# Output stage on grid columns, with the second Fourier step tile by tile

## The reference

```python
q, k, v, gA, bB, cB, hB, gB, uC, gC, qD, kD, vD, gD, aF, aB = split(hN @ w_in)
yA = attention(q, k, v) * silu(gA)           # 8 x 16 window of the grid, and 512 cached keys
yB = bB * conv3(cB * hB) * silu(gB)          # along the tokens, rows of the grid one after the other
yC = real(fft2(uC over tokens, over 64 channels)) * silu(gC)
yD = rms_norm(scan_forward + scan_backward) * silu(gD)
y  = x + gate * (concat(yA, yB, yC, yD) @ w_out)
```

## Time and profile before

| | us |
|---|---|
| median of 3 runs | 2692.43 (2691.7 to 2694.59) |
| the profiled execution | 2692.42 |
| its span, first to last instruction | 2690.7 |
| TensorE busy in it | 2508.2 (93%) |
| DVE, ACT, POOL busy | 1258.3, 990.2, 747.9 |
| DMA traffic | 395.37 MB, mean 147 GB/s |

### The profile page before, as it was taken

One profiled execution on the slowest core, in us unless ns is written; L12 is line 12 of the kernel. 1 busy time (PEld: TensorE's weight loads), 2 busy tenths in 40 slices (PEclk: granted clock), 3 DMA queues, 4 the chain that ended last, 5 costly groups with the idle time before them and its releaser, 6 DMA issues. The chain is left out here.

```text
span 2690.7 us, 53206 instructions
## 1 busy us (share of the span) xinstructions
PE 2508.2 (93%) x18956; PEld 2033.1 (76%) x18956; DVE 1258.3 (47%) x2620; ACT 990.2 (37%) x2031; POOL 747.9 (28%) x1147
## 2 busy tenths in 40 slices
PE   3899999999999969999999996989899985999999
PEld 1788888888888748888888885777777763888887
DVE  2544344344344343232323224667676753665654
ACT  1544544544444432222222213556565642111110
POOL 2233333333333210000000003433233332444442
PEclk8999999999999979999999998999999997999999
DMA  7533433433433362222222218887677768666563
GB/s 294 162 106 123 129 107 121 124 110 124 120 116 116 93 237 95 84 95 82 96 82 96 89 54 164 173 180 166 156 167 166 192 172 312 217 209 208 200 214 129
DMA packets 270748, 395.37 MB, mean 147 GB/s; under 512 B 43061, under 2 KB 192501, under 8 KB 268427
## 3 DMA queue, kind: packets, MB, share of 16 engines
q1 hardware_dynamic: 256252, 367.26, 47.1%
q10 hardware_dynamic: 13743, 25.02, 2.6%
q0 software_dynamic: 608, 1.12, 0.1%
HBM read 267.35 MB, written 125.96 MB: 146 GB/s over the span
## 5 line engine op out<-in xcount | busy, mean ns | idle before, releaser
L260 PE MATMUL p_ps_m<-p_w_hi,p_h_hi 128*128 128x512 f32 x1904 | 769.8, 404 | 15.9 <-DVE p_h_lo L876 13.3
L262 PE MATMUL p_ps_m<-p_w_hi,p_h_lo 128*128 128x512 f32 x1904 | 746.9, 392 | 0.0
L261 PE MATMUL p_ps_m<-p_w_lo,p_h_hi 128*128 128x512 f32 x1904 | 745.9, 392 | 0.0
L260 PEld LDWEIGHTS p_ps_m<-p_w_hi,p_h_hi 128*128 128x128 f32 x1904 | 360.1, 189 | 87.9 <-issue 14.0
L262 PEld LDWEIGHTS p_ps_m<-p_w_hi,p_h_lo 128*128 128x128 f32 x1904 | 359.2, 189 | 78.2
L261 PEld LDWEIGHTS p_ps_m<-p_w_lo,p_h_hi 128*128 128x128 f32 x1904 | 360.3, 189 | 69.2
L260 PE MATMUL o_ps_y<-o_w_hi,o_y_hi 128*128 128x512 f32 x544 | 217.9, 401 | 4.7 <-DVE o_w_lo L1862 4.7
L261 PE MATMUL o_ps_y<-o_w_lo,o_y_hi 128*128 128x512 f32 x544 | 217.6, 400 | 0.0
L262 PE MATMUL o_ps_y<-o_w_hi,o_y_lo 128*128 128x512 f32 x544 | 214.2, 394 | 0.0
L564 POOL TENSOR_TENSOR p_ve<-p_ss,p_eps 128x1 f32<-128x1 f32 x68 | 13.5, 199 | 597.2 <-ACT p_xr L630 597.2
L867 DVE TENSOR_TENSOR p_xt<-p_xt,p_ps_r 128x1024 f32<-128x1024 f32 x68 | 82.7, 1216 | 191.0 <-PE p_ps_r L748 191.0
(11 more groups left out here) (219 smaller groups left out, 4379.2 us busy)
## 6 DMA issues: line engine op xcount, KB each, us to landing
a_scan<-s_scan SPq DMA_DIRECT2D x68, 258.0 KB, 6.0
a_kv<-s_kv SPq DMA_DIRECT2D x68, 256.0 KB, 7.5
s_scan<-p_w_raw SPq DMA_DIRECT2D x134, 128.0 KB, 2.4
a_v_win<-s_p SPq DMA_DIRECT2D x132, 128.0 KB
p_xr<-in_x_sample SPq DMA_DIRECT2D x32, 512.0 KB, 3.9
p_xt<-in_x_sample_t SPq DMA_DIRECT2D x32, 512.0 KB, 4.6
p_xr<-in_x_columns SPq DMA_DIRECT2D x32, 512.0 KB, 10.1
p_xt<-in_x_columns_t SPq DMA_DIRECT2D x32, 512.0 KB, 10.8
```

The lines of the kernel that those rows point to most:

```text
L260: pe.matmul(out, left_hi(k), right_hi(k), start=(k == 0), stop=False)
L261: pe.matmul(out, left_hi(k), right_lo(k), start=False, stop=False)
L262: last = pe.matmul(out, left_lo(k), right_hi(k), start=False, stop=(k == K8 - 1))
```

## The change

- The Fourier stage is gone, and yc with it. y1 is laid out as (2, 64, 64, 256), and pass 1 sends it in two sends per tile.
- The output stage takes the grid by columns: tile t is grid columns 2t and 2t+1. od, conv_u, gbc, g_ad and ya are read by columns out of arrays in the order of tokens, x comes from `x_columns`, and y_sample is written by columns. Two new loads per tile: its y1 (`mid`) and its part of the table (`second`).
- PE does the second step of tile t+1 right behind the turn of tile t; DVE multiplies it with its gate straight out of PSUM, which POOL did. The prompt's product comes before tile 30. In front of each turn of a grid tile PE now waits for the loads of the tile after it.
- Four pieces of w_out are read in the attention stage at tiles 26 to 29, in place of y1 and the table.
- The first two tiles and the first four pieces of w_in for pass 0 are read in the modulation stage, behind w_mod.
- Small buffers are allocated last in several stages, and a scan buffer is 8 values longer.

```diff
@@ modulation_stage, sync
+            for t in range(2):
+                sp.dma_start(begun["xr"][t][:, :], io["x_sample"][0, t * P:(t + 1) * P, :]).then_inc(begun_in, 16)
+                sp.dma_start(begun["xt"][t][:, :, :], io["x_sample_t"][t]).then_inc(begun_in, 16)
+            for n, (k, nk, c0, wd, _, _) in enumerate(weight_pieces(PASS_BLOCKS[0])[:4]):
+                sp.dma_start(begun["w_raw"][n][:, 0:nk * wd].rearrange("p (k n) -> p k n", k=nk),
+                             io["w_in"][0, k * P:(k + nk) * P, c0:c0 + wd].rearrange("(k p) n -> p k n", p=P)).then_inc(begun_in, 16)
             sp.wait_ge(rows_sb, BLOCKS)
...
+            sp.wait_ge(begun_in, 8 * 16)
@@ projection_stage, send_columns
                 for r in range(2):
-                    for z in range(2):
-                        sp.dma_start(io["y1"][:, r, bass.ds(2 * t, 2)][:, z], y_sb[s][64 * r:64 * r + 64, z, :]).then_inc(y_sent[s], 16)
+                    sp.dma_start(io["y1"][r, bass.ds(2 * t, 2)].rearrange("b k c -> k b c"), y_sb[s][64 * r:64 * r + 64, :, :]).then_inc(y_sent[s], 16)
@@ attention_scan_stage
-        scan = two("scan", [P, 3 * 512 + 8])
+        scan = two("scan", [P, 3 * 512 + 16])
...
                 if isinstance(i, int) and 26 <= i < 30:
-                    g = i - 26
-                    sp.dma_start(fourier["mid"][:, 8 * g:8 * g + 8, :], io["y1"][g].rearrange("r b q c -> (r b) q c")).then_inc(fourier_in, 16)
-                if isinstance(i, int) and i == 30:
-                    sp.dma_start(fourier["second"][:, :, :], io["dft_second"]).then_inc(fourier_in, 16)
+                    sp.dma_start(stage_w[i - 26][:, :, :], out_piece(io, i - 26)).then_inc(stage_w_in, 16)
@@ output_stage
+    columns = lambda a, t: a.rearrange("(r w) c -> w r c", w=GRID_W)[bass.ds(2 * t, 2)]
...
+                sp.dma_start(mid[s][:, :, :], io["y1"][:, :, bass.ds(2 * t, 2), :].rearrange("r q k c -> (r q) k c")).then_inc(mix_in[s], 16)
+                sp.dma_start(second[s][:, :, :], io["dft_second"][:, bass.ds(2 * t, 2), :]).then_inc(mix_in[s], 16)
                 for d in range(2):
-                    sp.dma_start(od[s][:, d, :], io["od"][d, bass.ds(tok, P), :]).then_inc(mix_in[s], 16)
+                    sp.dma_start(od[s][:, d, :], columns(io["od"][d, 0:N_GRID, :], t)).then_inc(mix_in[s], 16)
                 for a in range(3):
-                    sp.dma_start(u[s][:, a, :], io["conv_u"][bass.ds(tok + (SKIP[j] - 1 + a), P), :]).then_inc(mix_in[s], 16)
+                    sp.dma_start(u[s][:, a, :], columns(io["conv_u"][SKIP[0] - 1 + a:SKIP[0] - 1 + a + N_GRID, :], t)).then_inc(mix_in[s], 16)
+                sp.dma_start(gbc[s][:, :, :].rearrange("p a c -> p (a c)"), columns(io["gates_bc"][0:N_GRID, :], t)).then_inc(mix_in[s], 16)
+                sp.dma_start(g_ad[s][:, :, :].rearrange("p a c -> p (a c)"), columns(io["p1"][0:N_GRID, P1_G:P1_W], t)).then_inc(mix_in[s], 16)
+                sp.dma_start(ya[s][:, :], columns(io["ya"][0:N_GRID, :], t)).then_inc(mix_in[s], 16)
...
             load_mix(0, 0)
-            load_weights(range(4))
             load_mix(1, 1)
...
-                sp.dma_start(x[s][:, :], token_rows(io, "x_sample", "x_prompt", t, j)).then_inc(x_in[s], 16)
+                sp.dma_start(x[s][:, :], token_rows(io, "x_columns", "x_prompt", t, j)).then_inc(x_in[s], 16)
@@ output_stage, gpsimd
-                pool.tensor_tensor(mix[s][:, 2, :], gbc[s][:, 1, :], yc[s][:, :], ALU.mult)
@@ output_stage, scalar
-                act.dma_start(token_rows(io, "y_sample", "y_prompt", t, j), y[s][:, :]).then_inc(sent[s], 16)
+                to = token_rows(io, "y_sample", "y_prompt", t, j) if j else columns(io["y_sample"][0], t)
+                act.dma_start(to, y[s][:, :]).then_inc(sent[s], 16)
@@ output_stage, tensor
+            def second_step(t, s):
+                for b in range(2):
+                    last = pe.matmul(ps_f[64 * b:64 * b + 64, s, :], second[s][:, b, :], mid[s][:, b, :], start=True, stop=True)
+                last.then_inc(four_mm, 1)
+
             def turn(t, s, _):
                 pe.wait_ge(mixed, t + 2)
                 pe.wait_ge(lo_done, t * 2 + 2)
+                if not isinstance(t, int) or t + 1 < GRID_T:
+                    pe.wait_ge(mix_in[1 - s], (t + 1 - (1 - s)) * (LOADS * 8) + LOADS * 16)
+                    pe.wait_ge(conv_done, t + 2)
...
+                if not isinstance(t, int) or t + 1 < GRID_T:
+                    second_step(t + 1, 1 - s)
@@ output_stage, vector, combine
+                dve.wait_ge(turned, t * 2 + 2)
+                if kind(t):
+                    dve.wait_ge(prompt_mm, 1)
+                    dve.tensor_tensor(mix[s][:, 2, :], ps_p[:, t - GRID_T, :], gbc[s][:, 1, :], ALU.mult)
+                else:
+                    dve.wait_ge(four_mm, t + 1)
+                    dve.tensor_tensor(mix[s][:, 2, :], ps_f[:, s, :], gbc[s][:, 1, :], ALU.mult)
```

More of the change, by code:

```diff
@@ L346, in projection_stage @@
         if which == 0:
[L347 to L349 removed]
+            rows = begun["rows"]
+            w_raw = begun["w_raw"]
             gqk = sb("gqk", [P, 2 * NH * HD])
@@ L396, in projection_stage @@
             early_in = sem("early_in")
+        ss, ve, rstd = ([sb(f"{n}{s}", [P, 1]) for s in range(2)] for n in ("ss", "ve", "rstd"))
+        half_pow = sb("half_pow", [P, 8])
+        eps = sb("eps", [P, 9])
         block = ctx.enter_context(nc.Block())
@@ L857, in _ @@
                 dve.sem_inc(rows_sent[s], 16)
+            if begun:
+                for s in range(2):
+                    dve.sem_inc(xr_in[s], 16)
+                    dve.sem_inc(xt_in[s], 16)
+                for s in range(4):
+                    dve.sem_inc(w_in[s], 16)
             if which == 0:
@@ L1641, in output_stage @@
         w_lo = sb("w_lo", [P, K8, DM], F32R)
-        stage_w = [sb(f"stage_w{s}", [P, 2, 512]) for s in range(4)]
+        y_hi = two("y_hi", [P, K8, P], F32R)
+        y_lo = two("y_lo", [P, K8, P], F32R)
         gate = sb("gate", [P, 2, DM])
@@ L1652, in output_stage @@
         gbc = two("gbc", [P, 2, W_GRP])
-        yc = two("yc", [P, W_GRP])
+        mid = two("mid", [P, 2, W_GRP])
+        second = two("second", [P, 2, 64])
+        whole = sb("whole", [P, 2, 2, N_PROMPT])
+        gp = sb("gp", [P, 2, 2, W_GRP])
         od = two("od", [P, 2, W_GRP])
@@ L1727, in _ @@
             pool.sem_inc(mixed, 1)
+            for part in range(2):
+                pool.dma_start(gp[:, part, :, :], io["g"][part].rearrange("(j p) c -> p j c", p=P)).then_inc(prompt_in, 16)
+                pool.dma_start(whole[:, part, :, :], io["dft_whole"][part].rearrange("(j p) k -> p j k", p=P)).then_inc(prompt_in, 16)
             pool.wait_ge(gn_done, 1)
@@ L1810, in turn @@
                     last.then_inc(turned, 1)
+                if not isinstance(t, int) or t + 1 < GRID_T:
+                    second_step(t + 1, 1 - s)
+            pe.wait_ge(mix_in[0], LOADS * 16)
+            second_step(0, 0)
             turn(0, 0, 0)
             for t, s, j in tile_pairs(pe):
+                if isinstance(t, int) and t == GRID_T - 2:
+                    pe.wait_ge(prompt_in, 64)
+                    for kc in range(2):
+                        for r in range(2):
+                            for m in range(2):
+                                last = pe.matmul(ps_p[:, kc, :], whole[:, r, m, kc * P:(kc + 1) * P], gp[:, r, m, :],
+                                                 start=(r == 0 and m == 0), stop=(r == 1 and m == 1))
+                    last.then_inc(prompt_mm, 1)
                 pe.wait_ge(lo_done, t * 2 + 4)
@@ L1892, in build @@
         keep = {"ident": sb("ident", [P, P]), "mod": sb("mod", [P, 2, K8, 2])}
-        modulation_stage(nc, io, keep)
-        projection_stage(nc, io, keep, 0)
+        with ExitStack() as inner:
+            begin = lambda name, shape: inner.enter_context(nc.sbuf_tensor("b_" + name, shape, F32))
+            begun = {"xr": [begin(f"xr{s}", [P, DM]) for s in range(2)], "xt": [begin(f"xt{s}", [P, K8, P]) for s in range(2)],
+                     "rows": [begin(f"rows{s}", [P, R_W]) for s in range(2)]}
+            begun["w_raw"] = [begin(f"w_raw{s}", [P, 1024]) for s in range(2)] + [begun["rows"][s][:, 0:1024] for s in range(2)]
+            modulation_stage(nc, io, keep, begun)
+            projection_stage(nc, io, keep, 0, begun)
         with ExitStack() as inner:
```

185 lines of the change are left out of this document (57 added, 128 removed).

## The result

The changed kernel takes 3518.03 us (median of 4 runs, 3515.39 to 3522.03), the kernel before 2692.37 beside it: ratio 1.3054, 95% interval 1.3035 to 1.3072. Forecast were 3486 us, 3400 to 3580 for the likeliest case and 3180 to 3600 with the case of a second pair. The change costs 826 us, all of it in the output stage: that stage begins at 2219.70 us, where the Fourier stage began before (2219.48).

The account below looks back on a forecast made before the run. Bound: one DMA engine pair in the output stage. Third load set landed at 2314.0, plus 29 x 38.2 to 3421.8, plus 59.1 and 3.7 gives 3484.6; -0.6 elsewhere gives 3484.0 span, 3486 us; range 3180 to 3600.

Parts of the forecast that it names:

- the likeliest case: Output stage: column reads and the write share one pair of DMA engines; 3486 us, range 3400 to 3580, chance 0.76.
- the case of a second pair: Output stage: the write of y_sample has its own engine pair; 28.3 us per tile, 3199 us, chance 0.10.
- The mechanism: Output stage: column transfers of outermost size 2 run on 2 of 16 DMA engines, at 48 to 53 GB/s.
- The tile: Output stage's loop: 27.1 us for one set of loads, 38.2 us per tile in all with the write.
- The write on the same pair: Output stage: the y_sample write on ACT's queue uses the same engine pair as the reads, 9.9 us per tile.
- The head: Output stage's start: begins at 2219.5 us, two load sets in by 2275.7, third issued at 2283.2, landed at 2314.0.
- The tail: Output stage's end: 59.1 us after the turn of tile 30, plus 3.7 us for the prompt product.
- Hidden work: Output stage: TensorE's second step, 0.49 us per tile, is hidden by DMA; VectorE's multiply, 0.3 to 0.5 us, costs nothing.
- The other stages: Modulation's early loads and projection net -0.6 us (ends +3 and -3); pass 1 0; attention 0 (-18 to +18).
- The rival on the other side: Output stage: column reads spread over all 16 engines after all; -6.5 us, 2686 us, chance 0.08.

Follow-up runs that it names:

- split_all: The changed kernel with every column read and write cut in two, one per grid column (outermost size 64); 2722.51 us, ratio 1.0097.
- interleaved: The changed kernel with grid rows outermost and the 2 columns behind them, second-step table padded with zeros, no splitting; 2697.05 us, ratio 1.0000.
- two and four runs: The kernel before, od and u read as 2 runs of 64 rows: 2945.74 us; or all nine loads but x as 4 runs of 32: 2894.21 us.
- split_write: The changed kernel with only the write of y_sample cut into its two columns; 3264.56 us, ratio 1.2106.
- split_merged: split_all with its bytes in 12 loads per tile, od's two directions in one and u's three taps as 3 KB rows; 2703.53 us, ratio 1.0026.
- before_two_runs: The kernel before with grid tiles' od and u read as 2 runs of 64 neighbouring rows; 2945.74 us, ratio 1.0924.

## Why the prediction was right

**The mechanism.** Column transfers run on two engines whichever way they go, reads as the writes of pass 1 did: shown by the share of 0.13 in the loop, by the two queues that together keep 2 engines busy, by the cure (split_all, interleaved) and by the counter-test in the kernel before (two and four runs). The reading of 0.13 and 0.28 as 2 and 4 of 16 was the step on which all hung.

**The tile.** 38.2 forecast; turn 1 to turn 30 took (3450.90 - 2324.84) / 29 = 38.83, or 18 us over 29 tiles. The rates were 48 and 51 to 53 GB/s as put in; 52 for the longer rows gives 38.6.

**The write on the same pair.** Taken so without a row of ACT's, at 0.10 for the rival; the two queues' shares in the changed kernel and split_write show it.

**The head.** The stage began at 2219.70 (forecast 2219.5). The first turn came at 2283.29, 7.6 us later than forecast: POOL's 1 MB for the prompt is in flight then, a term that I left out, and if it spreads over all 16 engines, which no run shows, its eighth costs the pair 131,072 B / 53 = 2.5 us (an estimate). The rest, some 5 us, I can't divide; the sum's 2 us of latency, for which no row was named, is in the same stretch. The gap from there to the third set's issue was 7.34 us (7.5). That set took 34.2 us to land where 30.8 were put down (turn 1 at 2324.84, forecast 2314.0); of the 10.8 us that this makes, 7.6 are the first turn's and 3.4 are new.

**The tail.** 64.4 for 62.8. Sum of the misses: 10.8 + 18.3 + 1.6 = 30.7, against 3515.3 - 3484.0 = 31.3.

**Hidden work.** DVE's multiply out of PSUM took 418 ns (0.3 to 0.5 forecast) and cost nothing. The second step took 1.12 us per tile at the lower clock, and under the transfers that cost nothing; with the cover gone it was 0.52 us per tile (12.60 - 12.08 in split_merged), or 0.59 in the form with zeros (0.49 forecast).

**The other stages.** Wrong in sign, by 1.5 us: projection pass 0 began at 48.19 us (forecast 47.9) and its first square no longer waited (50.81 for 51.22), but what lies between the square and the first product took 1.3 us longer (61.84 for 60.92): +0.9 for -0.6. The forecast stopped at the square. Attention: TensorE's wait for kv 15.9 for 18.3, the stage's end the same.

**The rival on the other side** was priced at 2686 if the reads spread. Built, it measured 2697.05, ratio 1.0000, or by the profiled executions 3.1 us of span behind before in place of 6.5 ahead. Of these 9.6 us the waits at the head make 4.5 (+9.7 for 5.2) and turns 1 to 30 with the second step 3.4 (+19.0 for 15.6; the step took 0.59 us for 0.49). The rest, 1.7, is in the small terms, the first issue's -28.7 for -29.9 above all.

## What to carry to other kernels

Before a layout change, write down the outermost size of each DMA's access pattern on both sides: it was the number of engines that a DMA got here, for sizes 2 and 4, at 23 to 26 GB/s each, and all those of size 2 shared the same two, from both queues. The cure is to turn the dimensions round (one product against a table with zeros paid for it here) rather than to split, as the issuing engine has its own limit: SP's 19 issues took 12.8 us in a tile of split_all. A stage that is taken away gives back only what its work doesn't cost on the engine that bounds the loop it moves into: of 28.7 us, 22 came back on TensorE and the rest, with more, in the head, which had to be ordered anew.

## What the runs showed of the hardware that I had not expected

- While narrow transfers are outstanding, the engine that issues is held up. One issue took 14.20 us; all issues of ya (shortest, median and longest, in ns), in the changed kernel and in interleaved:

```profile
2843.12 14.20 SPq L1643 DMA_DIRECT2D o_ya<-s_ya  x1
...
L1643 SPq DMA_DIRECT2D o_ya<-s_ya x32: 4339/13456/15212, 2239.6 to 3427.2; - x32
```

```profile
L1643 SPq DMA_DIRECT2D o_ya<-s_ya x32: 554/555/1469, 2227.9 to 2620.8; - x32
```

- Spread loads behind them in the queue are held up too, although 14 engines are free: the issue of x, which spreads, took 4.9 us at the median in the changed kernel and 0.55 in interleaved. Those of mid and second, which follow x, stayed at 0.33.

- TensorE's granted clock fell from 1.00 to 0.68 in a loop that leaves it idle for 24 us before each turn; a turn of eight behind such a wait takes 1.97 us, nearly twice the 1.04 of a TensorE that was busy before it, so it runs at the 1.2 GHz level; later in the product the clock rises again (one matmul takes 0.63 us at first and 0.40 from then on). In interleaved, busy throughout, it is 1.00.
- The distance between the rows of a column transfer (64 KB for od, more for the gates) cost nothing that shows on two engines: the pair moved 48 GB/s in od's rows and 46 in rows that lie next to each other (before_two_runs).
